# Value pages issued by GpSimd, in one order with the key pages, and SyncE left with the weights

## What is computed

```
def stick_breaking_block(q, k, v, q_pos, k_pos, offset):
    z = (jnp.einsum('bqhd,bshd->bhqs', q, k) * (q.shape[-1] ** -0.5)
         + offset.astype(jnp.float32)[None, :, None, None])
    ...
    log_beta = jax.nn.log_sigmoid(z)
    log_rest = jnp.where(mask, jax.nn.log_sigmoid(-z), 0.0)
    between = lax.cumsum(log_rest, axis=3, reverse=True) - log_rest
    weight = jnp.where(mask, jnp.exp(log_beta + between), 0.0)
    return jnp.einsum('bhqs,bshd->bqhd', weight, v)

        k_past = cache_k[i][page_table].reshape(dec_b, n_past, HC, DC)
        v_past = cache_v[i][page_table].reshape(dec_b, n_past, HC, DC)
```

## Time and profile before

| | |
|---|---|
| median of 3 runs | 2438.76 us (2429.02 to 2443.66) |
| profiled execution | 2441.72 us, span 2440.2 us, mean granted TensorE clock 0.947 |
| PE busy | 2238.2 us (92%) |
| DVE busy | 1161.6 us (48%) |
| ACT, POOL busy | 598.4 us (25%), 192.3 us (8%) |
| queue q1 (SP), q0 (POOL) | 311.99 MB, 113.67 MB |

### The profile page before, as it was taken

The page is one execution under the profiler, slowest core; times in us unless marked ns, Lnnn a source line. Parts: engine busy times, 40 slices in busy tenths (PEclk is TensorE's granted clock), DMA queues, the critical chain, the costliest instruction groups (busy, mean ns, idle before and its releaser), DMA issues.

```text
span 2440.2 us, 45909 instructions
## 1 busy us (share of the span) xinstructions
PE 2238.2 (92%) x17191; PEld 1977.7 (81%) x17191; DVE 1161.6 (48%) x3560; ACT 598.4 (25%) x741; POOL 192.3 (8%) x301
## 2 busy tenths in 40 slices
PE   6799999999998989689979987999999998999997
PEld 2189888888887978689968887888788787788997
DVE  1542333424243343434363256776677766755332
ACT  1322121212122121222232232232222222233221
POOL 0000101101010101000000001011011011000110
PEclk9899899989999899879989999999999999999999
DMA  9977454545645464223442245777878877854442
GB/s 317 315 218 214 141 173 155 150 147 160 192 148 164 133 182 155 71 73 110 119 143 75 73 122 200 261 254 257 268 244 270 274 239 240 267 181 130 135 130 61
DMA packets 400019, 437.02 MB, mean 179 GB/s; under 512 B 16916, under 2 KB 306990, under 8 KB 399167
## 3 DMA queue, kind: packets, MB, share of 16 engines
q1 hardware_dynamic: 359270, 311.99, 41.9%
q0 software_dynamic: 30752, 113.67, 13.4%
q10 hardware_dynamic: 9810, 8.73, 1.1%
HBM read 407.79 MB, written 26.54 MB: 178 GB/s over the span
## 4 chain that ended last, share of the span: by engine, by line
PE 66%; DVE 15%; DMA 8%; issue 5%; ACT 4%; POOLq 1%; POOL 0%; DVEq 0%; SPq 0%; ACTq 0%
PE pt L507 50%; PE m L507 14%; DMA arena<-in_cache_k 6%; DVE arena L1636 4%; ACT arena L916 2%; ACT w_hi L916 2%; DVE w_lo L1276 1%; DMA raw<-in_e_w_ada 1%; PE m L511 1%; DMA arena<-in_o_k_norm_g 1%; POOLq L1878 1%; DVE arena L1447 1%; PE pt L511 0%; DVE arena L1794 0%; DVE arena L1393 0%
## 5 line engine op out<-in xcount | busy, mean ns | idle before, releaser
L507 PE MATMUL pt<-act_hi,w_hi 128*128 128x260 f32 x4384 | 924.1, 293 | 63.6 <-DVE act_lo L1359 23.2
L507 PE MATMUL pt<-act_hi,w_lo 128*128 128x260 f32 x4384 | 897.0, 287 | 0.0
L507 PE MATMUL pt<-act_lo,w_hi 128*128 128x260 f32 x4384 | 896.7, 287 | 0.0
L507 PEld LDWEIGHTS pt<-act_hi,w_hi 128*128 128x128 f32 x4384 | 693.1, 194 | 126.5 <-issue 96.8
L1276 DVE TENSOR_TENSOR w_lo<-raw,w_hi 128x1024 fp32r<-128x1024 f32 x274 | 335.3, 1224 | 906.7 <-ACT w_hi L916 906.2
L507 PEld LDWEIGHTS pt<-act_lo,w_hi 128*128 128x128 f32 x4384 | 693.2, 193 | 0.0
L507 PEld LDWEIGHTS pt<-act_hi,w_lo 128*128 128x128 f32 x4384 | 691.0, 193 | 0.0
L916 ACT ACTIVATE w_hi<-raw 128x1024 fp32r<-128x1024 f32 x274 | 289.6, 1057 | 1170.3 <-PE pt L507 1155.0
L1636 DVE CUSTOM_DVE_ANT_0 arena<-arena 128x128 f32<-128x128 f32 x1024 | 224.9, 286 | 104.8 <-DMA arena<-in_cache_k 104.5
L916 ACT ACTIVATE arena<-arena 128x1040 f32<-128x1040 f32 (+8 forms) x199 | 169.7, 864 | 281.2 <-DVE arena L1730 81.7
L507 PE MATMUL m<-arena 128*128 128x128 f32 (+7 forms) x1136 | 210.0, 348 | 6.9 <-POOL arena L1939 4.1
(11 more groups left out here) (161 smaller groups left out, 1096.6 us busy)
## 6 DMA issues: line engine op xcount, KB each, us to landing
arena<-in_cache_k POOLq DMA_DIRECT2D x128, 512.0 KB, 4.9
arena<-in_cache_v SPq DMA_DIRECT2D x128, 512.0 KB, 5.1
raw<-in_o_w_in SPq DMA_DIRECT2D x112, 512.0 KB, 5.6
raw<-in_e_w_in SPq DMA_DIRECT2D x98, 512.0 KB, 4.4
raw<-in_e_w_ada SPq DMA_DIRECT2D x96, 512.0 KB, 5.7
raw<-in_o_w_ada SPq DMA_DIRECT2D x96, 512.0 KB, 5.4
raw<-in_e_w_out SPq DMA_DIRECT2D x32, 512.0 KB, 4.1
raw<-in_o_w_out SPq DMA_DIRECT2D x32, 512.0 KB, 4.8
```

The lines of the kernel that those rows point to most:

```text
L507: return pe.matmul(out, lhsT, rhs, start=start, stop=stop, skip_group_check=True)
```

## The change

The value pages leave SP's list and enter POOL's. Slots, semaphores, sizes and readers stay as they are. SP's list in l1b has only the weight units left. POOL's list is written per pass b: key pages 0 and 1 of sample b + 1, the queries, the head's weights, value pages 1, 2, 0 of sample b, and then for n from 1 to 9 the two key pages that step n's reading makes room for (if n is one of `KEYS_AT`) followed, from n = 3 on, by value pages 2n - 3 and 2n - 2. The last pass has no keys.

```diff
@@ SP's list
-            def value_page(b, p):
-                first = isinstance(b, int) and b == 0
-                if p >= 3:
-                    sp.wait_ge(s("v_free"), b * 16 + (p - 2))
-                elif not first:
-                    sp.wait_ge(s("v_free"), b * 16 - (0, 2, 1)[p])
-                page = sp.value_load(ptab[0:1, bass.ds(b * NPAGE + p, 1)], min_val=0, max_val=NPOOL - 1)
-                sp.dma_start(pages[:, value_slot(p), :], cv[bass.ds(page, 1)].rearrange("n s d -> (n s) d"))\
-                    .then_inc(s(f"page{value_slot(p)}"), 16)
...
-                    if at_ == 0:
-                        for p in (1, 2, 0):
-                            value_page(i, p)
-                    if at_ >= 3:
-                        for p in (2 * at_ - 3, 2 * at_ - 2):
-                            if p < NPAGE:
-                                value_page(i, p)
-
-            sp.wait_ge(s("ptab"), 16)
@@ POOL's list
+            def value_page(b, p):
+                first = isinstance(b, int) and b == 0
+                if p >= 3:
+                    pool.wait_ge(s("v_free"), b * 16 + (p - 2))
+                    pool.sem_inc(s("pool_waited"), 1)
...
+                page = pool.value_load(ptab[0:1, bass.ds(b * NPAGE + p, 1)], min_val=0, max_val=NPOOL - 1)
+                pool.dma_start(pages[:, value_slot(p), :], cv[bass.ds(page, 1)].rearrange("n s d -> (n s) d"))\
+                    .then_inc(s(f"page{value_slot(p)}"), 16)
...
+            def sample(b, keys=True):
+                if keys:
+                    key_page(b + 1, 0)
+                    key_page(b + 1, 1)
+                    queries(b + 1)
+                head_weights(b)
+                for p in (1, 2, 0):
+                    value_page(b, p)
+                for n in range(1, 10):
+                    if keys and n in KEYS_AT:
+                        k = KEYS_AT.index(n)
+                        for p in (2 * k + 2, 2 * k + 3):
+                            if p < NPAGE:
+                                key_page(b + 1, p)
+                    if n >= 3:
+                        for p in (2 * n - 3, 2 * n - 2):
+                            if p < NPAGE:
+                                value_page(b, p)
...
-            sample_keys(0)
-            sample_keys(1)
-            with pool.Fori(2, NB) as b:
-                sample_keys(b)
-            head_weights(HC - 1)
+            first_keys()
+            sample(0)
+            with pool.Fori(1, NB - 1) as b:
+                sample(b)
+            sample(NB - 1, False)
```

More of the change, by code:

```diff
@@ L434, in _ @@
                 weights("l1a", j, L1A_ORDER, v["o_w_in"], l1a_cols(j))
-            cv = a["cache_v"][0].rearrange("n s h d -> n s (h d)")
             def l1b_load(i, u):
@@ L1880, in key_page @@
                     .then_inc(s(f"page{key_slot(p)}"), 16)
+            cv = a["cache_v"][0].rearrange("n s h d -> n s (h d)")
+            def value_page(b, p):
[3 more added lines that the diff above has]
+                    pool.sem_inc(s("pool_waited"), 1)
+                elif not first:
+                    pool.wait_ge(s("v_free"), b * 16 - (0, 2, 1)[p])
+                    pool.sem_inc(s("pool_waited"), 1)
+                page = pool.value_load(ptab[0:1, bass.ds(b * NPAGE + p, 1)], min_val=0, max_val=NPOOL - 1)
+                pool.dma_start(pages[:, value_slot(p), :], cv[bass.ds(page, 1)].rearrange("n s d -> (n s) d"))\
+                    .then_inc(s(f"page{value_slot(p)}"), 16)
             def queries(b):
@@ L1891, in head_weights, with first_keys @@
                 pool.dma_start(brow[0:1, 0:P], a["o_b_s"][0, bass.ds(h, 1)]).then_inc(s("ws_in"), 16)
-            def sample_keys(b):
+            def first_keys():
                 for p in range(NPAGE):
-                    key_page(b, p)
+                    key_page(0, p)
                     if p == 1:
[L1897 to L1901, removed]
-            sample_keys(0)
-            sample_keys(1)
-            with pool.Fori(2, NB) as b:
-                sample_keys(b)
-            head_weights(HC - 1)
+                        pool.wait_ge(s("q_out"), 16)
+                        queries(0)
+            def sample(b, keys=True):
[21 more added lines that the diff above has]
+            sample(NB - 1, False)
         @block.gpsimd
```

## The result

The changed kernel takes 2645.83 us in the median of four executions (2626.08 to 2654.71), beside 2438.65 for the kernel before (four, 2429.02 to 2443.66). The ratio is 1.0817, with a 95% interval of 1.0767 to 1.0867: 8% slower. The profiled execution took 2654.71 us, of which 2653.2 are the span. In the code after, PE's matmuls are L487, `w_lo` is L1256, the reading of key pages L1616, POOL's key pages L1859 and its value pages L1873.

The account below looks back on a forecast made before the run. PE, busy 92% of the span, was taken to bound the kernel. 19.6 us idle plus 4.5 clock give 24.1 in each of seven passes, 169 on 2441.7: 2611, less 3 for the median, 2608 us; range 2545 to 2680.

Parts of the forecast that it names:

- What bounds, and who covers SP: In l1b PE is busy 688 of 735 us; nobody waits for SP's weights; 128 issues added to POOL, 147 us, hide.
- The new wait: In l1b, PE's next step waits for DVE's reading: handoff 7.3 us, four waits of 3.3 to 7.8 per pass.
- The third rival, Less of it: In l1b, landings near 3.6, DVE done with step 3 at 6.0, clock holds: 13.3 us per pass, 2532 us; chance 0.12.
- Idle time of the pass: In l1b, a pass takes 109.4 us in place of 89.8: 19.6 more in each of seven passes.
- The clock: PE's clock in l1b falls after four waits: 6.0 us, less 1.5 already paid, so 4.5 per pass.
- Faster: In l1b, keys land earlier and DVE's waits for them go: at most 37 us gained, 2402 us; chance 0.04.
- No change: In l1b, PE's slack of 47 us takes the new waits, or DVE runs ahead: 2439 us; chance 0.04.
- More of it: In l1b, POOL's descriptors wait behind DVE's instruction, some 1.5 us on each of four handoffs: 42 more, 2650 us; chance 0.12.

Follow-up runs that it names:

- the kernel with values first: Changed kernel, but in POOL's list the two value pages stand ahead of the two key pages at each place n: 2412.20 us, ratio 0.9858.
- the filled kernel: Changed kernel plus idle matmuls on PE between the two value pages of steps 4, 6, 8 and 10, first seven passes: 2598.07 us, ratio 1.0622.

## Why the prediction was right, point by point

**What bounds, and who covers SP.** Held. SP has no wait for `v_free` left, and no engine gained by it. The 128 issues on POOL are hidden: 142 us busy in l1b, and the kernel with values first has the same.

**The new wait.** Held in place, in count and in size: 24.8 per pass were forecast, 174 in all, in steps 4, 6, 8 and 10; 174.2 were measured in 28. In sample 4 the four are 7.35, 2.90, 6.29 and 9.54, for 7.4, 3.3, 6.3 and 7.8. Counted from the value read of step 3, PE reads page 3 at 16.1 (forecast 15.6), and page 15 at 91.4 (forecast 82.8, before any price of the clock). That the total agrees to 0.2 is luck: its parts were off and cancelled. The time from DVE's last reading to the value issue held (2.7, for 1.5 and 1.15). The awaited landings are 6.3, 5.3, 5.2 and 6.5 and not 4.6; at pages 3 and 15 a weight unit goes out at the same moment, which is 1.2 and 1.7 of them. Against that DVE ended step 3 of sample 4 at 7.1 and not at 8.3. By the timelines, what had put it back in the kernel before was a key page in step 10 of the pass ahead, for which DVE waited 1.9 until 1871.0; the same step had no such wait here. The third rival had 6.0 for this, so about half of that part came. The chain of waits of the kernel after, sample 4, shows the four landings and what PE did behind them; x48 is a unit, x28 half a value read and `between`, x32 half a value read and the other matmuls of step 10:

```profile
2028.80 6.32 DMA arena<-in_cache_v
2035.17 1.04 PE m L487 x8
2036.21 8.04 PE pt L487 x48
...
2053.24 5.01 DMA arena<-in_cache_v
2058.29 1.04 PE m L487 x8
2059.33 6.84 PE pt L487 x48
...
2074.57 5.31 DMA arena<-in_cache_v
2079.93 7.68 PE m L487 x28
...
2103.19 7.16 DMA arena<-in_cache_v
2110.40 8.75 PE m L487 x32
2119.20 7.51 PE pt L487 x48
```

**Idle time of the pass.** 19.6 more per pass, 137 in all, was forecast; 142 was measured in l1b.

**The clock.** The mis-sized term: "Four waits of 3.3 to 7.8 make 6.0, less the 1.5 that the present one costs: 4.5". It came from one row, `between` after one wait of 4.3. Measured are 63 / 7 = 9.0 per pass. The chain above and two rows of PE's timeline, the first ten records of step 10 behind the value read (before, sample 3; after, sample 4), say where the rest is:

```profile
1864.44 2.65 PE L507 MATMUL m<-arena 128*128 128x512 f32 x10
```

```profile
2111.37 4.87 PE L487 MATMUL m<-arena 128*128 128x512 f32 x10
```

In sample 4 each half value read behind a wait takes 1.04 in place of 0.62, 0.4 more. The unit behind page 3 takes 8.04, against 5.94 undisturbed, 2.1 more; the one behind page 7 0.9 more. Behind page 11 `between` takes 6.7 (the 7.68 less 1.0), against 4.6, 2.1 more. Behind page 15, the longest wait, the ten records take 2.2 more and the unit after them 1.6. With the four 0.4 that is 10.6, less the 1.5 that `between` cost before: 9.1. So the waits cost 2.5, 1.3, 2.5 and 4.2, and not 1.5 each: the price of one wait of 4.3 with few matmuls behind it was applied to waits of up to 9.5 and to waits with 48 matmuls close behind. The term is 7 x 4.5 = 32 us short, and with the 5 by which the idle time was short that is nearly all of 2646 - 2608 = 38. The Trainium skill, "TensorE: Matmul & The Clock Gate", "Why this matters for your kernels", tells to avoid idle gaps between bursts of matmuls for this reason; the filled kernel agrees, with 0.98 in place of 0.86.

**The rivals.** *Faster* did not come: its condition, a value page in time despite the key page ahead, failed in all seven passes. The gain that it named exists in the other order, 2412 measured for the 2402 it gave. *No change* fell with the idle time of 142. *Less of it* had two of its three parts wrong: landings were not near 3.6, and the clock did not hold. *More of it* gave 2650, closer to the measured 2646 than the forecast, by a mechanism that the runs don't support: it put 42 us more into the waits, which came out at 174.2 for 174, and the awaited pages take as long when SP issues them. The Trainium skill, "SBUF — State Buffer", "SBUF: two separate sides", warns that descriptors of GpSimd's transfers can't be written while DVE runs an operation in a mode that takes the port pair the two share. No run here shows such a delay, and in the kernel with values first the pages of POOL cost PE 5.2 us in all. That descriptors were never held up was not shown directly, and neither was whether DVE's instructions here are of that kind.

## What to carry to other kernels

A list of transfers that one engine issues in order joins the consumers of all its entries: before an entry is put behind another, ask which condition comes first in time, and put that one ahead. Two pairs of entries swapped at each place were worth 234 us of 2646 here, while a change of the engine alone was worth 1.4% at most in POOL's favour (2412 against 2439, uncoupled) and 2% in SP's (2592 against 2646, coupled). When a new wait falls on TensorE, price the matmuls behind it at the lower clock as well, for as long as rows at that clock show it and not by one short group.

## What was not expected of the hardware

- Four waits of 3 to 10 us per pass cost 9.0 us of longer matmuls per pass, a third on top of the waits. Adding 137 us of matmuls whose result nothing reads made the changed kernel 48 us faster.
- A 512 KB page landed in 3.4 us at least in the kernel before, and in 5.2 to 6.5 on average where PE waited for it; holding back one weight unit of the same size that had started with it took 1.2 to 1.7 off.
- With key and value pages in one list and the values ahead, DVE's waits for key pages halved (100.8 to 50.3 us), though no key page was issued on an earlier condition. The cause is open.
